# The norms between the stages of a two-layer decoder kernel: by halves of a token tile, with Sqrt and a reciprocal, transposes in a pipeline, and two weight splits moved behind them

## The reference

```python
def rms_norm(x, gain):
    y = xf * lax.rsqrt(jnp.mean(xf * xf, axis=-1, keepdims=True) + EPS)
    return (y * gain.astype(jnp.float32)).astype(x.dtype)
...
for layer in range(DEPTH):                       # DEPTH = 2
    h = rms_norm(x, mix_norm[layer])
    if layer % 2 == 0:
        z = h @ ab_w_in[j]                       # attention q, k, v and a convolution's input
        ...
        x = x + jnp.concatenate([a, c], axis=-1) @ ab_w_out[j]
        h = rms_norm(x, ffn_norm[layer])
        x = x + swiglu(h, ffn_w_in[j], ffn_w_out[j])          # width 2816
    else:
        o = hgrn2(h @ hgrn_w_in[j], lb_all[j], hgrn_norm[j])  # gated linear recurrence
        x = x + o @ hgrn_w_out[j]
        h = rms_norm(x, ffn_norm[layer])
        x = x + moe_swiglu(h, moe_router[j], moe_w_in[j], moe_w_out[j])  # top 2 of 8 experts
```

## Time and profile before

| | |
|---|---|
| median of 3 runs | 1646.61 us (1645.4 to 1649.04) |
| the profiled execution's span, first to last instruction | 1645.1 us |
| PE busy | 1545.1 us (94%) |
| DVE busy | 1241.0 us (75%) |
| ACT busy | 1011.3 us (61%) |
| POOL busy | 145.4 us (9%) |
| DMA | 429.21 MB, 261 GB/s over the span |
| mean granted TensorE clock | 0.973 |

### The profile page before, as it was taken

How to read it: one execution, slowest core, us unless ns; L and a number is a source line. 1 busy time by engine, 2 the same in 40 slices (tenths; PEclk the granted TensorE clock), 3 DMA queues, 4 the chain that set the end, 5 groups by cost and what they waited for, 6 DMA issues and landing times.

```text
span 1645.1 us, 28853 instructions
## 1 busy us (share of the span) xinstructions
PE 1545.1 (94%) x10932; PEld 1429.3 (87%) x10932; DVE 1241.0 (75%) x1144; ACT 1011.3 (61%) x960; POOL 145.4 (9%) x184
## 2 busy tenths in 40 slices
PE   6779899998999779999999999999999999999997
PEld 6747799998998679989989989989998998998996
DVE  5974544446466678888888879879888878888887
ACT  5347533446454647767767766766766766776775
POOL 4546000000034210000000000000000000000000
PEclk9868899999999989999999999999999999999999
DMA  9320455564630339999999999999999999999994
GB/s 294 122 77 26 144 189 180 190 185 123 191 129 1 122 107 362 361 309 347 359 310 349 356 316 343 360 323 334 359 334 324 359 355 303 359 359 305 356 356 157
DMA packets 322805, 429.21 MB, mean 261 GB/s; under 512 B 6753, under 2 KB 288538, under 8 KB 322762
## 3 DMA queue, kind: packets, MB, share of 16 engines
q1 hardware_dynamic: 322400, 427.93, 76.6%
q0 software_dynamic: 320, 0.69, 0.2%
q10 hardware_dynamic: 42, 0.01, 0.0%
HBM read 427.55 MB, written 1.05 MB: 261 GB/s over the span
## 4 chain that ended last, share of the span: by engine, by line
PE 66%; DVE 2%; issue 2%; ACT 1%; DVEq 0%; ACTq 0%
PE bank L1226 20%; PE bank L1228 19%; PE bank L1227 19%; PE bank L1544 2%; PE bank L1466 2%; PE bank L1578 1%; PE bank L1561 1%; PE bank L1562 0%; DVE hs_l L823 0%; DVE w_l L247 0%; PE bank L1448 0%; PE bank L1447 0%; ACT w_h L242 0%; PE bank L1479 0%; DVE ma_l L832 0%
## 5 line engine op out<-in xcount | busy, mean ns | idle before, releaser
L247 DVE TENSOR_TENSOR w_l<-raw,w_h 128x2048 fp32r<-128x2048 f32 x396 | 906.9, 2295 | 250.4 <-ACT w_h L242 246.6
L242 ACT ACTIVATE w_h<-raw 128x2048 fp32r<-128x2048 f32 x406 | 775.1, 1912 | 180.9 <-PE bank L1228 180.9
L1226 PE MATMUL bank<-w_h,hs_h 128*128 128x256 f32 x1792 | 515.1, 287 | 1.4 <-DVE hs_l L823 1.4
L1228 PE MATMUL bank<-w_h,hs_l 128*128 128x256 f32 x1792 | 505.2, 282 | 0.0
L1227 PE MATMUL bank<-w_l,hs_h 128*128 128x256 f32 x1792 | 504.2, 281 | 0.0
L1227 PEld LDWEIGHTS bank<-w_l,hs_h 128*128 128x128 f32 x1792 | 338.6, 189 | 4.9
L1226 PEld LDWEIGHTS bank<-w_h,hs_h 128*128 128x128 f32 x1792 | 336.3, 188 | 6.2 <-issue 1.6
L1228 PEld LDWEIGHTS bank<-w_h,hs_l 128*128 128x128 f32 x1792 | 337.7, 188 | 0.0
L1226 PE MATMUL bank<-h_h,w_h 128*128 128x256 f32 x672 | 195.7, 291 | 17.1 <-DVE conv_in L504 11.2
L1227 PE MATMUL bank<-h_l,w_h 128*128 128x256 f32 x672 | 193.7, 288 | 0.0
L1228 PE MATMUL bank<-h_h,w_l 128*128 128x256 f32 x672 | 193.6, 288 | 0.0
(11 more groups left out here) (276 smaller groups left out, 1558.3 us busy)
## 6 DMA issues: line engine op xcount, KB each, us to landing
raw<-in_moe_w_in SPq DMA_DIRECT2D x227, 1024.0 KB, 5.1
raw<-in_moe_w_out SPq DMA_DIRECT2D x112, 1024.0 KB, 5.3
raw<-in_ffn_w_in SPq DMA_DIRECT2D x22, 1024.0 KB, 5.1
raw<-in_hgrn_w_in SPq DMA_DIRECT2D x16, 1024.0 KB, 5.5
raw<-in_ffn_w_out SPq DMA_DIRECT2D x11, 1024.0 KB, 4.8
raw<-in_ab_w_in SPq DMA_DIRECT2D x10, 1024.0 KB, 11.3
raw<-in_ab_w_out SPq DMA_DIRECT2D x4, 1024.0 KB, 4.8
raw<-in_hgrn_w_out SPq DMA_DIRECT2D x4, 1024.0 KB, 4.9
```

The lines of the kernel that those rows point to most:

```text
L242: act.activation(w_h[:, u0 % S, :], raw[:, u0 % R, :], ACT.Copy).then_inc(w_high, 1)
L247: eng.tensor_tensor(w_l[:, u0 % S, :], raw[:, u0 % R, :], w_h[:, u0 % S, :], ALU.subtract).then_inc(w_low_pool if POOL_FROM <= u0 < POOL_T ...
L1226: pe.matmul(o, a_high, b_high, start=start, stop=False, skip_group_check=True)
L1228: return pe.matmul(o, a_low, b_high, start=False, stop=stop, skip_group_check=True)
```

## The change

What it does, part by part:

1. **The last unit tile by tile.** In a stage's last output unit PE goes by tile, then half, then chunk, so that the four banks are complete one after the other, and o_part rises three times instead of once. DVE's add_part adds each of them as it is done.
2. **Squares by halves.** ACT squares 128 x 512 at a time, with a sum for each half: four instructions instead of two.
3. **Sqrt and reciprocal.** DVE's norm_eps makes sum0/D + EPS, ACT takes Sqrt(sum1/D + that) for one tile, and DVE takes the reciprocal. One table serves squares, Sqrt and the gains' copies; Ln, Exp and the table load between them are gone. There are 29 table loads in the program before and 26 now.
4. **Scaling by halves**, tile 0 while tile 1 is still being squared, in the order that residual_norm writes out.
5. **Transposes in a pipeline.** PE waits for halves of a tile, and three and four keep_warm matmuls (128 x 512, bfloat16, result unused) stand before and between the tiles' transposes in norms 1 to 3.
6. **Splits and tables later.** norm_high comes ahead of ACT's next table load and of its split of the third unit. norm_low comes ahead of DVE's low parts of both the second and the third unit (before, the second's was made ahead of the norm). Norm 0 has the same parts but no fillers, and its Sigmoid table load stands behind norm_high.

The core of the diff:

```diff
+WARM = (0, 4, 4, 4)
...
-            for u in range(U_AB_OUT, U_FFN - 1):
+            for u in range(U_AB_OUT, U_FFN - 2):
                 split_low(dve, u + 3)
-            residual(U_FFN)
-            norm_scale(1)
+            residual_norm(1)
+            norm_low(1, C_FFN)
+            split_low(dve, U_FFN + 1)
             split_low(dve, U_FFN + 2)
-            norm_low(1, C_FFN)
...
+            def norm_eps(n, tt):
+                dve.wait_ge(n_sq, 4 * n + 2 * tt + 1)
+                dve.tensor_scalar(n_stat[:, n, 2, tt:tt + 1], n_stat[:, n, 0, tt:tt + 1], 1.0 / D, EPS, ALU.mult, ALU.add).then_inc(n_eps, 1)
+            def norm_scale(n, tt):
+                dve.wait_ge(n_rms, TT * n + tt + 1)
+                dve.reciprocal(n_stat[:, n, 4, tt:tt + 1], n_stat[:, n, 3, tt:tt + 1]).then_inc(n_rs, 1)
+                dve.wait_ge(n_rs, TT * n + tt + 1)
+                for half in range(2):
+                    v = slice(half * 512, (half + 1) * 512)
+                    dve.tensor_scalar(xn[:, tt, v], x[:, tt, v], n_stat[:, n, 4, tt:tt + 1], None, ALU.mult).then_inc(n_xn, 1)
+            def residual_norm(n):
+                add_part(n, 0, 0)
+                add_part(n, 0, 1)
+                norm_eps(n, 0)
+                add_part(n, 1, 0)
+                norm_scale(n, 0)
+                add_part(n, 1, 1)
+                norm_eps(n, 1)
+                norm_scale(n, 1)
...
+                if last_unit:
+                    for tt in range(TT):
+                        for half in range(2):
+                            for c in range(OC):
+                                last = part(c, tt, half)
+                            if tt + half < 2:
+                                last.then_inc(o_part, 1)
...
             def norm_turn(n):
+                if n:
+                    keep_warm(3, 3)
+                    pe.wait_ge(x_add, 4 * n)
                 for tt in range(TT):
-                    pe.wait_ge(n_xn, TT * n + tt + 1)
                     for j in range(4):
+                        if j % 2 == 0:
+                            pe.wait_ge(n_xn, 2 * (TT * n + tt) + j // 2 + 1)
...
+                    if tt == 0:
+                        keep_warm(WARM[n], 4 if n == 3 else 3)
```

More of the change, by code:

```diff
@@ L99, in build @@
         eps = sb("eps", [P, 1])
-        n_stat = sb("n_stat", [P, 4, 3, TT])
+        n_stat = sb("n_stat", [P, 4, 5, TT])
         router = sb("router", [P, KC, NE])
@@ L166, in build @@
         const, dve_const = sem("const"), sem("dve_const")
-        n_sq, n_ln, n_rs, n_xn, n_t, n_high, n_low = (sem(f"n_{k}") for k in "sq ln rs xn t high low".split())
+        n_sq, n_eps, n_rms, n_rs, n_xn, n_t, n_high, n_low = (
+            sem(f"n_{k}") for k in "sq eps rms rs xn t high low".split())
         o_part, x_add = sem("o_part"), sem("x_add")
@@ L468, in norm_low @@
                                                  op0=ALU.mult, op1=ALU.subtract).then_inc(n_low, 1)
-            def residual(units):
-                for tt in range(TT):
-                    if tt == 0:
-                        dve.wait_ge(o_part, {U_FFN: 1, U_HG_IN: 2, U_MOE: 3}[units])
-                    else:
-                        dve.wait_ge(w_used, units)
-                    for half in range(2):
-                        v = x[:, tt, half * 512:(half + 1) * 512]
-                        dve.tensor_tensor(v, bank[:, 4 + 2 * tt + half, :], v, ALU.add).then_inc(x_add, 1)
-            norm_scale(0)
+            for tt in range(TT):
+                norm_eps(0, tt)
+            for tt in range(TT):
+                norm_scale(0, tt)
             split_low(dve, 0)
@@ L751, in _ @@
             hg_low(3)
-            for u in range(U_HG_OUT, U_MOE - 1):
+            for u in range(U_HG_OUT, U_MOE - 2):
                 split_low(dve, u + 3)
-            residual(U_MOE)
-            norm_scale(3)
+            residual_norm(3)
+            norm_low(3, C_FFN + 8)
+            split_low(dve, U_MOE + 1)
             split_low(dve, U_MOE + 2)
-            norm_low(3, C_FFN + 8)
             done = [0]
@@ L951, in _ @@
             norm_sums(0)
-            table(ACT.Sigmoid)
             split_high(act, 0)
             norm_high(0, C_MIX)
+            table(ACT.Sigmoid)
             split_high(act, 1)
```

71 lines of the change are left out of this document (40 added, 31 removed).

## The result

| | before | after |
|---|---|---|
| median | 1646.95 us (4 runs, 1645.4 to 1649.04) | 1609.68 us (4 runs, 1607.76 to 1612.87) |
| ratio, 95% interval | | 0.9776 [0.9761, 0.9791] |
| span of the profiled execution | 1645.1 us | 1609.0 us |
| mean granted TensorE clock | 0.973 | 0.979 |

The change makes the kernel 37 us faster. The forecast was 1632.2 us with a range of 1628.5 to 1639.5, so it had the sign right and missed the size by 22 us. The page of the changed kernel, part 1, answers to the earlier trace rows: PE is busy for 20 us less, although it has seven more fillers at each of three norms.

What follows compares the result with a forecast made beforehand. PE was busy 94% of the span, so time could come only from its waits or half clock, at the norms' serial chains. 1.1 + 6.6 + 6.7 + 0 = 14.4 us off 1645.1, plus 1.5 for the median: 1632.2 us, range 1628.5 to 1639.5.

Steps and rivals of the forecast that it cites:

- Norms 1 and 2: Transitions behind these norms: shorter serial chain and full clock gain 6.6 us at norm 1 and 6.7 at norm 2.
- The rival of the clock that still falls: Norms 1 and 2: PE still drops to 1.2 GHz, costing 3.1 us a norm; chance 0.13 for one or both.
- Norm 0: First norm: same chain, limited by the first weight unit landing at 9.9 us; gain 1.1 us, bounds 0 and 1.9.
- Norm 3: Norm ahead of the router: shorter chain offset by two DVE splits ahead of the logits' copy; 0, bounds +2.0 and -3.4.
- The sign that was named for this: Norm 3: one POOL operation's length (2.11 us) would show inside one of DVE's two splits.
- So the shift passes through to the end: Behind norm 2: engine-to-engine chains to 595 us, then experts with PE busy throughout, keep the gained time; no loss forecast.
- The experts' stage at 1050 us, as before: Experts' loop at the end: its length stays 1050 us, gain 0.
- The range: Whole kernel, 1628.5 to 1639.5 us: below, norms 3 and 0 at best plus 0.9; above, both norms cold, norm 0 losing 1.

Runs made afterwards that it cites:

- e11: Changed kernel with part 6 undone at norms 1 and 2 (splits and table load back ahead of gains, adds and h_l): 1626.01 us, ratio 0.986.
- e10: Changed kernel without its fillers (keep_warm matmuls) in norms 1 to 3: 1609.54 us, ratio 0.9766.
- e13: Changed kernel with DVE's two splits of norm 3 moved behind the first gather: 1607.76 us, ratio 0.9759.
- e8: Changed kernel with n_stat at 256 bytes a partition instead of 160, moving every tensor behind it: 1600.44 us, ratio 0.9722.
- e1: Kernel before with only n_stat widened from 96 to 160 bytes, so tensors behind it start 64 bytes further on: 1629.8 us, ratio 0.9885.
- e2: Changed kernel with n_stat kept at 96 bytes, so every tensor starts where it did before: 1627.37 us, ratio 0.9872.
- e6: Kernel before with n_stat at 128 bytes, plus six one-column memsets at the start of DVE's stream: 1622.97 us, ratio 0.9847.
- e9: Bench of matmul groups scanning the distance between stationary and moving operands' starts in 32-byte steps, nothing else running: 0.1174 to 0.1200 us for 256 columns.
- e7: Kernel before with measured matmuls behind its end, operand starts varied, alone and beside DVE, ACT and weight loads: first group 0.1199 us each.
- e14: The bench scanning operand distance, in finer steps of 4 bytes for 256 columns and 8 for 512: 0.1333 us at 28, 32 and 36 bytes.
- e3: Kernel before with n_stat at 128 bytes, so all tensors behind it move by 32 bytes: 1629.0 us, ratio 0.9884.
- e16: Kernel before with n_stat at 128 bytes, plus two tiny memsets at DVE's start: 1628.7 us, one run.
- e17: Kernel before with n_stat at 128 bytes, plus four tiny memsets at DVE's start: 1626.9 us, one run.

## Why the prediction was wrong

- **Norms 1 and 2, right:** 6.6 and 6.7 us, both as forecast, with the distance of 5.58 us (5.5) and clock 1.00. The terms, though, hung on the splits: with them back in place (e11) norm 1 lost 7.0 us and norm 2 6.3, about all that the two had gained. The rival of the clock that still falls did not come; e10 puts what the fillers hold off at 0 and 0.6 us.
- **Norm 0, mis-sized:** 0.2 us instead of 1.1. ACT's split of the first unit started at 10.84 us, when the first load landed, and not at 9.9, the landing in the trace of before, on which the term rested. In the kernels of this study the first gain starts anywhere from 14.7 to 18.5 us, whatever the order, so a gain of 1 us there could not have been told in one trace.
- **Norm 3, right in sum, by another way:** the chain up to h_l is 5.1 us shorter, and the router's path lost 5.5; the "0" was two real terms that cancel, and e13 takes 3.1 of the loss away. The copy of the logits lost 3.1 us against h_l, and the chain behind it 2.4 more. The sign that was named for this did not come: the two splits took 4.48 us together, so neither was blocked by POOL. POOL was held instead (its pair of differences took 6.71 us where it took 4.22), ended later, and made one more small operation of the router's chain take 2.04 us instead of 0.17.
- **"So the shift passes through to the end", wrong in the recurrence too:** 2.9 us of it were lost between PE's second unit behind norm 2 and the stage's last matmul. That stretch took 172.0 us before and 174.9 after, but 172.0 to 173.7 in the kernels with the order of before, and 172.0 in e8 with the order of after. So the order of work does not set it; which waits do was not tried.
- **"The experts' stage at 1050 us, as before": the step that failed**, for 16.4 of the 22 us. It took 1033.6. The prediction costed every instruction of the diff and gave its one changed allocation nothing, not even a bound. The passage "a loop with PE busy throughout, so the shift passes through to the end" took a busy PE for a PE at its limit. 5376 matmuls with hs went from 0.1199 to 0.1169 us, which is some 16 us; e1 and e2 show that the place of the operands does it.
- **The first stage, nothing forecast, for 8.6:** the prediction followed the shift of norm 0 (1 us) and took later waits as fixed. The trace of before had the row of 5.81 us for two operations of 0.7, a wait on POOL that a shift of one engine against another by 1 us removes. It was not priced. The shift came from the faster loop ahead of it, which e6 puts down to six instructions more in DVE's stream; no row of before could have told that.
- **The range** was the sum of the bounds of the steps that were seen. Nothing in it stood for what the change moves without naming it, and its lower end, 1628.5, is still 1 us above what e2 gives without the moved tensors (1627.4), which is the first stage's doing.

## What to carry to other kernels

When PE's busy time in a stretch differs and its count doesn't, compare from start to start, and look at what moved in SBUF: the distance between the starts of the stationary and the moving operand, modulo 256 bytes, is a tuning knob worth 27 us of 1627 here (e2 against e8, which run the same instructions in the same order), and an added scratch column turns it by accident. Before crediting a change with a gain, and before calling any one part of it useful (e11), run it with its allocations held in place (e2), and the old order with the new ones (e1). Price every place where two engines start a shared turn within a microsecond of each other: a small shift anywhere before it gains or loses the whole turn.

## What the runs showed of the hardware

- The pace of matmuls back to back depends on the distance of the operands' starts modulo 256 bytes. At the eight multiples of 32 it was 0.1174 to 0.1200 us for 256 columns and 0.2267 to 0.2340 for 512 (e9), at full clock. Of these eight, 0 is among the worst for 256 columns and the best for 512. DVE, ACT and DMA traffic at 282 GB/s beside it changed nothing (e7).
- At some distances there are two paces (0.1135 and 0.1178 at 64, 0.1182 and 0.1333 at 32) which last for a whole group or unit (e9, e14, e8).
- A loop on DVE of two operations took 1.065 us a round with none or two, 1.09 with four and 0.86 with six tiny instructions added at the start of the program, some 90 us earlier (e3, e16, e17, e6).
- Two DVE operations of 0.7 us took 5.81 us together where a POOL operation of 4.49 us began at the same moment, and 1.41 where they had begun ahead of it.
- Of two gaps of PE of the same make, 16 transposes and no fillers, one kept the full clock and one lost it (e10).
